# Output-weight rests moved to GpSimd, reciprocals that write the spread tile, sinks added by columns: a two-block transformer kernel on one core

## The reference, cut to what matters

```
denom = jnp.sum(p, axis=-1, keepdims=True) + jnp.exp(sink_l - m)
return jnp.einsum('bkrqj,bjkd->bqkrd', (p / denom).astype(vb.dtype), vb)
```

## Time and profile before

| | |
|---|---|
| median of 3 runs | 2412.17 us (2411.51 to 2412.3) |
| the profiled execution | span 2412.2 us |
| PE busy | 2293.1 us (95%) |
| DVE busy | 1721.1 us (71%) |
| ACT busy | 1338.0 us (55%) |
| POOL busy | 653.4 us (27%) |
| sparse attention's `over` tiles | 419 to 743 us |
| latent attention | about 975 to 1340 us |
| Fourier part | about 1560 to 1582 us |
| windowed attention | 1582 to 1761 us |

### The profile page before, as it was taken

One profiled execution on the slowest core, in us unless ns is written; L12 is line 12 of the kernel. 1 busy time (PEld: TensorE's weight loads), 2 busy tenths in 40 slices (PEclk: granted clock), 3 DMA queues, 4 the chain that ended last, 5 costly groups with the idle time before them and its releaser, 6 DMA issues. The chain is left out here.

```text
span 2412.2 us, 36011 instructions
## 1 busy us (share of the span) xinstructions
PE 2293.1 (95%) x13399; PEld 1787.5 (74%) x13399; DVE 1721.1 (71%) x3317; ACT 1338.0 (55%) x2172; POOL 653.4 (27%) x576
## 2 busy tenths in 40 slices
PE   9999999899999999999998999989967999999998
PEld 7687887555656987777777889767746888888886
DVE  4899995677774225666677456477766988889887
ACT  5646212455555375555655443455554777777774
POOL 2446211011010000766677600002223112212211
PEclk9999999999999999999999999999978999999999
DMA  4121214011013332233333431121146999999996
GB/s 159 35 80 62 80 51 135 31 53 49 32 47 105 86 75 64 75 85 83 85 117 96 143 136 58 42 96 54 36 171 272 389 383 383 392 392 382 383 397 194
DMA packets 163110, 361.09 MB, mean 150 GB/s; under 512 B 34944, under 2 KB 82768, under 8 KB 162940
## 3 DMA queue, kind: packets, MB, share of 16 engines
q1 hardware_dynamic: 149564, 312.49, 35.8%
q0 software_dynamic: 13232, 46.25, 6.9%
q10 hardware_dynamic: 144, 0.07, 0.0%
HBM read 325.16 MB, written 38.86 MB: 151 GB/s over the span
## 5 line engine op out<-in xcount | busy, mean ns | idle before, releaser
L1344 ACT ACTIVATE a_pT<-ps 128x512 f32<-128x512 f32 (+3 forms) x176 | 79.5, 484 | 164.3 <-PE ps L1213 162.9
L4249 POOL DMA_INDIRECT out_dram<-m_q,e_token x15 | 35.7, 2383 | 443.9 <-DVE m_q L4452 443.9
L1356 ACT ACTIVATE a_p<-ps,a_stat 128x384 f32<-128x384 f32 (+7 forms) x192 | 129.1, 674 | 21.4 <-DVE a_stat L1440 15.3
L3150 ACT ACTIVATE l_lat<-ps,h_stat 128x384 f32<-128x384 f32 (+7 forms) x128 | 94.2, 741 | 78.1 <-DVE h_stat L3351 40.5
L2723 POOL TENSOR_TENSOR ada_acc<-ada_acc,ada_w 128x384 f32<-128x384 f32 x112 | 117.5, 1049 | 8.8
L1260 PE MATMUL ps<-l_wo,a_mixT 128*128 128x512 f32 x256 | 119.6, 593 | 0.0
L3160 ACT ACTIVATE h_pT<-ps 128x512 f32<-128x512 f32 (+2 forms) x192 | 83.5, 490 | 56.0 <-PE ps L3030 56.0
L4071 DVE TENSOR_TENSOR x_w2l<-x_raw,x_w2h 128x4096 fp32r<-128x4096 f32 x23 | 101.8, 4425 | 17.9 <-ACT x_w2h L4063 17.9
L4071 DVE TENSOR_TENSOR x_w1l<-x_raw,x_w1h 128x4096 fp32r<-128x4096 f32 x23 | 101.8, 4425 | 16.0 <-ACT x_w1h L4063 16.0
L4063 ACT ACTIVATE x_w2h<-x_raw 128x4096 fp32r<-128x4096 f32 x24 | 87.2, 3635 | 42.0 <-PE ps L4286 36.1
L4071 DVE TENSOR_TENSOR x_w0l<-x_raw,x_w0h 128x4096 fp32r<-128x4096 f32 x23 | 101.8, 4424 | 8.3 <-ACT x_w0h L4063 8.0
(11 more groups left out here) (778 smaller groups left out, 7149.4 us busy)
## 6 DMA issues: line engine op xcount, KB each, us to landing
x_raw<-in_w_gate SPq DMA_DIRECT2D x25, 2048.0 KB, 11.3
x_raw<-in_w_down SPq DMA_DIRECT2D x24, 2048.0 KB, 10.3
x_raw<-in_w_up SPq DMA_DIRECT2D x23, 2048.0 KB, 12.0
ada_w<-in_w_ada POOLq DMA_DIRECT2D x64, 384.0 KB, 3.7
m_ufT<-in_w_up SPq DMA_DIRECT2D x9, 2048.0 KB, 11.8
m_ufT<-in_w_down SPq DMA_DIRECT2D x8, 2048.0 KB, 13.3
l_raw<-in_e_w_in SPq DMA_DIRECT2D x28, 512.0 KB, 3.7
m_ufT<-in_w_gate SPq DMA_DIRECT2D x7, 2048.0 KB, 10.3
```

Of the source, the lines that this page charges most:

```text
L1356: nc.scalar.activation(self.p[2 * (u % 2) + side][:, 0:pair.width], self.S(u, side)[:, 0:pair.width], ACT.Exp, bias=self.stat[:, 1, s], sc ...
L3150: self.nc.scalar.activation(p[:, 0:w].rearrange("p (i n) -> p i n", i=2) if w > 512 else p[:, 0:w], self.S(u, side), ACT.Exp, bias=self.st ...
```

## The change

It has four parts.

1. In the latent attention and in `PairAttention` the reciprocal reads the two sums with a step of zero and writes the 128x128 tile `over` itself. The 128x2 reciprocal, the wait behind it and the copy are gone.
2. The sinks are added by two instructions of 128x1, with one wait behind both, in place of one of 128x2.
3. At the end of the Fourier stage, two of the four rests of the first half of `w_out` (the first two of `LATE`) go to GpSimd, which waits for `router.ready` first; two stay on DVE.
4. In the windowed attention all four rests of the second half go to GpSimd, ahead of its other work.

```
         if pair.maps[side].sink is not None:
-            link(nc.vector.tensor_tensor(st[:, 2, both], st[:, 2, both], st[:, 4, both], ALU.add))
-        link(nc.vector.reciprocal(st[:, 3, both], st[:, 2, both]))
-        nc.vector.tensor_copy(self.over[u % 2][:].rearrange("p (i n) -> p i n", i=2),
-                              st[:, 3, both].unsqueeze(2).broadcast_to([P, 2, 64])).then_inc(self.inverse, 1)
+            for c in (s.start - 1, s.start):
+                link.note(nc.vector.tensor_tensor(st[:, 2, c:c + 1], st[:, 2, c:c + 1], st[:, 4, c:c + 1], ALU.add))
+            link.wait()
+        nc.vector.reciprocal(self.over[u % 2][:].rearrange("p (i n) -> p i n", i=2),
+                             st[:, 2, both].unsqueeze(2).broadcast_to([P, 2, 64])).then_inc(self.inverse, 1)
...
+    def pool_rests(self, e):
+        for c in range(KD // 2):
+            e.wait_ge(self.highs, c + 1)
+            self.nc.gpsimd.tensor_tensor(self.low[:, c, :], self.raw[:, c, :], self.high[:, c, :].bitcast(F32), ALU.subtract).then_inc(self.lows, 1)
+
     def dve(self, e, at, u):
-        if 0 < u <= KD // 2:
-            e.wait_ge(self.highs, u)
-            self.nc.vector.tensor_tensor(self.low[:, u - 1, :], self.raw[:, u - 1, :], self.high[:, u - 1, :].bitcast(F32), ALU.subtract).then_inc(self.lows, 1)
...
     def dve_norm(self, e, u):
         V, both = self.nc.vector, slice(2 * u % 8, 2 * u % 8 + 2)
         e.wait_ge(self.exped, 2 * u + 2)
-        self.link(V.reciprocal(self.stat[:, 3, both], self.stat[:, 2, both]))
-        V.tensor_copy(self.over[u % 2].rearrange("p (i n) -> p i n", i=2),
-                      self.stat[:, 3, both].unsqueeze(2).broadcast_to([P, 2, 64])).then_inc(self.inverse, 1)
+        V.reciprocal(self.over[u % 2].rearrange("p (i n) -> p i n", i=2),
+                     self.stat[:, 2, both].unsqueeze(2).broadcast_to([P, 2, 64])).then_inc(self.inverse, 1)
...
                     if p == PAIRS - 1 and not odd:
-                        low(3)
+                        low(e, nc.vector, 3)
                 if p == 1:
                     router.dve_start(e)
-                    low(0)
                 elif p == 2:
-                    low(1)
-                    low(2)
+                    low(e, nc.vector, 2)
+
+        @block.gpsimd
+        def _(e):
+            e.wait_ge(router.ready, 2)
+            for i in range(2):
+                low(e, nc.gpsimd, i)
...
         @block.gpsimd
         def _(e):
             e.wait_ge(w_in, 32)
+            split.pool_rests(e)
             for b in range(NB - 2):
                 at.pool(e, b)
```

More of the change, by code:

```diff
@@ L3798, in fourier_stage, with low @@
         block = scope.enter_context(nc.Block())
+        def low(e, engine, i):
+            c = LATE[i]
+            e.wait_ge(wo_highs, i + 1)
+            engine.tensor_tensor(wo_low[:, c, :], wo[:, c, :], wo_high[:, c, :].bitcast(F32), ALU.subtract)
         @block.sync
@@ L3810, in _ @@
             mirror_sums(nc, link, ufT[:, PAIRS - 1, :], router.junk).then_inc(last_summed, 1)
[L3811 to L3814, removed]
             for p in range(PAIRS):
```

## The result

The changed kernel takes 2417.49 us (median of 20 runs, 2414.69 to 2419.67) beside 2412.76 us for the kernel before (20 runs, 2407.72 to 2418.22). The ratio is 1.0017, its 95% interval 1.0011 to 1.0023: 2.7 to 5.5 us slower. The profiled execution took 2417.67 us, its span is 2415.8 us. The time lies inside the range of 2408.5 to 2421.5, 2.9 us above the point. It is outside the 2411 to 2417 of the forecast's own case and at the lower end of rival (2), 2417.4 to 2419.8.

A forecast was written before the change was run, and what follows sets the result against it. PE was taken to bound the latent and windowed attention, DVE the window's first steps and to finish last at the Fourier end. 2412.2 + 1.8 + 1.1 - 1.7 + 1.2 + 0 = 2414.6 us, range 2408.5 to 2421.5.

The forecast's parts named there:

- the forecast's own case: Whole kernel: the one-column sink adds are free of GpSimd; 2414.6 us, between 2411 and 2417, chance 0.5.
- rival (2): Window's first steps: one-column sink adds are held by GpSimd, +1.1 or +3.5 there; 2417.4 to 2419.8 us, chance 0.27.
- The rule that speaks against it: Sink adds: 128x1 taken as not held by column count, against the skill's rule that GpSimd shuts out two-SBUF-input DVE instructions.
- First steps: Window's start: three DVE rests saved (-3.66), less longer reciprocals (1.6) and second sink columns (0.2); -1.7 us.
- Latent attention: 64 units: the longer reciprocal delays PE at some of its eight waits for ACT's exponentials; +1.8 us, bounds 0 to 4.2.
- its eight chains: Latent attention's PE waits: four grow by some 0.5 us each, three gain nothing, the eighth is hidden by a hold.
- Sparse attention's start: First three units, from 419 us: two longer reciprocals lie ahead of PE's second wait; +1.1 us.
- Fourier end: End of the Fourier stage: DVE's own rest is held by GpSimd's second rest; +1.2 us, -0.85 without a hold.
- Window from 1606 us: Later windowed units: the stall moves from the copy to the mixed tile's rest, nothing won; 0 us.
- The price of the reciprocal: All 128 units: 957 ns for 128x128 from two measured rows, never held; an unheld pair becomes 0.53 us longer.

The follow-up runs named there:

- e5: The changed kernel with each sink added by a 128x1 tensor_scalar, the sink read as a per-partition scalar; 2413.7 us beside 2413.54 before, ratio 0.9999.
- e3: The changed kernel with the sinks added by one 128x2 instruction, as before; 2415.84 us beside 2412.51 for the kernel before, ratio 1.0014.
- e10: The changed kernel, its six rests kept on GpSimd, with pointer-scalar sink adds and the spread by a reduction; 2406.16 us beside 2412.93 before, ratio 0.9983.
- e1: The kernel before with only the reciprocals that write the spread tile, in all three attentions; 2417.03 us beside 2412.51, ratio 1.0017.
- e9: The kernel before with only the spreading copies made reductions over an axis of length one; 2410.88 us beside 2412.93, ratio 0.9990.
- e2: The changed kernel with the old reciprocal and copy and one 128x2 sink add, so only the six rests moved; 2415.77 us beside 2412.51 before, ratio 1.0009.
- e7: The kernel before with only the window's four rests on GpSimd and pointer-scalar 128x1 sink adds; 2411.45 us beside 2413.54, ratio 0.9987.
- e8: The kernel before with the window's four rests on GpSimd, pointer-scalar sink adds and the spread by a reduction; 2408.29 us beside 2413.54, ratio 0.9980.

## Why the prediction was right in its range and wrong in its mechanism

**The step that failed** is the one under "The rule that speaks against it": the adds of one column were taken as free because of the column count. They are held like two columns, as rival (2) had it. The pair in question took 1.91 us and e5's took 0.34 at the same place. With two tensor inputs the column count changes nothing (e3). The row that the count was taken from, the 128x1 instruction that stays at 214 to 216 in the earlier trace rows, has a single tensor input, and so has the 128x2 one above it that is held up to 2345: one column goes free there only together with one input. A pointer-scalar add of 128x2 was not tried. The Trainium skill's rule (SBUF — State Buffer, "SBUF: two separate sides") is the one that the traces bear out, down to one element for each partition and in both directions: in e5 it is GpSimd that is kept out.

**First steps**, -1.7 forecast, +1.2 measured. The rival's +1.1 is near, but its parts are not. The hold costs 2.0 us (e5), not 2.8: the first pair was held once, and the later ones took 0.36 and 0.44 in place of 0.23. Without it the forecast would still have been wrong by 1.0 (e5: -0.7), since the prediction took PE's idle time as time to be won. PE lost its idle time and did its work at a lower clock: 3.7 us more busy time in e10 against 4.8 less idle. Where this happens is seen in the matmuls that the kernel before ran from 1594.09 to 1602.30, here and then in e5 and e10:

```profile
1594.09:1602.30 8.21, 5.08 (x35) 2.55 (x34) 7.80 (x28) 5.58 (x16) 0.00 (x0) 0.99 0.00 0
```

```profile
1594.17:1602.40 8.23, 8.23 (x36) 4.01 (x36) 7.54 (x30) 5.44 (x17) 6.24 (x3) 0.50 0.19 78
```

```profile
1585.05:1593.19 8.14, 8.14 (x37) 4.00 (x36) 6.71 (x33) 5.46 (x17) 6.25 (x3) 0.50 0.15 60
```

In the kernel before DVE fills this stretch and PE idles at full clock. In e5 and e10 PE is busy throughout at 1.2 GHz, and the length is the same although DVE in e10 has 1.1 us less to do. Whether the longer stretch at 1.2 GHz follows from the lost idle time is not settled. The kernel before has 0.89 in its one profiled execution, and the change and the ten experiments have 0.77 to 0.83. e1 and e9 are among them with 0.77 and 0.79, though their rests are on DVE as before; PE idles for 4.8 us in e1, about as long as in the changed kernel. The clock of whole executions doesn't settle it either: its mean is 0.981 for the change, 0.982 to 0.983 for the kernel before, and 0.983 for e10.

**Latent attention**, +1.8 forecast. +1.2 in the pair of profiles and about 0.8 over those without the reduction. The term was sized too large by 0.6 to 1.0; which of its eight chains absorbed the rest was not tried.

**Sparse attention's start**, +1.1 forecast, +1.0 measured in the pair of profiles; the six with the long reciprocal have +0.9 to +2.0, the two highest of them at the lower clock. **Fourier end**, +1.2 forecast, +1.0 measured; the DVE rest took 2.96 us where 3.3 was named, since it arrived 1.9 us before GpSimd's end and needed only 1.10 after it.

**Window from 1606 us**, 0 forecast, -1.0 measured. That the stall only changes its place was right: L1613 is held in most of its eight. But a held instruction does part of its work while it stands: L1612 ended 0.68 us after GpSimd's instruction when it stood behind a held copy, L1613 in the block above ends 1757.08, 0.55 after it. That is 0.13 us for each of six blocks, 0.8 us together, and the shifts lie in those six blocks, 0.13 to 0.23 each. e1, e3 and e9 show the same -0.8 to -1.0, and e2, with the old pair, -0.1. (In e5, e7, e8 and e10, with their pointer sinks, the last of the six alone shifts by -1.25.)

**The price of the reciprocal**, 0.957 forecast from two rows, is 0.953; it is never held in these runs, as assumed.

**After 1760 us**, 0 forecast, -1.5 measured. Nothing of the change runs there, and the ten experiments have -0.1 to -2.4 in the same stretch, so this belongs to the single execution of before and not to the change.

The sum of the terms that are the change's own, +1.0 +0.8 +1.0 +1.2 -1.0 = +3.0 us, lies inside the timed interval of 2.7 to 5.5; with terms from single profiles the agreement is no finer than a microsecond. That the forecast's sum of +2.4 comes near it is partly luck: its first steps were 2.9 us too low, and its other terms together 2.3 us too high.

## What to carry to other kernels

A DVE instruction that has to run beside GpSimd should be chosen by form before size: here the two-input adds, the spreading copies and a one-input instruction of 128x2 were held. A 128x1 add with a pointer scalar in place of a second tensor and a reduction in place of a spreading copy are a little slower alone and were never held. Before work goes to GpSimd to free DVE, list the DVE instructions that will run during it and ask of each whether it will be held, and which one is late next. And PE's idle time is an upper bound of a gain at the same clock: read the granted clock of the stretch beside it.

## What the runs showed of the hardware that was not expected

- A two-input add of 128x1 is held as long as one of 128x2: 1844 and 1852 ns at most behind the first rest.
- The same add with a pointer scalar takes 206 ns in place of 158 when free, and 216 at most.
- A reduction over an axis of length one spreads 128x2 to 128x128 in 286 ns and is not held (291 at most in 128), against a copy's 227 that grows to 2370. The Trainium skill (VectorE: DVE Perf Modes, "The perf-mode tier table") gives a float32 copy from SBUF to SBUF twice the rate and a reduction only the plain one. The traces agree that the copy is the faster when free; at this size the plain form costs only 0.06 us more.
- A reciprocal's time grows by 6.3 ns for each output element, (953 - 202) / 120 between 128x8 and 128x128.
- A two-input instruction that waits behind GpSimd ends 0.55 us after it where it takes 0.63 alone.
